# One memory set for the two plain groups of each feed-forward block, squares added by transfers, and h's low part two steps later

## What is computed

```python
def rms_norm_2(x, gain):
    xf = x.astype(jnp.float32)
    inv = lax.rsqrt(jnp.mean(xf * xf, axis=-1, keepdims=True) + NORM_EPS)
    return (xf * inv).astype(x.dtype) * gain

def swiglu(h, w_gate, w_up, w_down):
    return (jax.nn.silu(h @ w_gate) * (h @ w_up)) @ w_down
...
    x = x + jnp.square(jax.nn.relu(h2 @ w_up[l])) @ w_down[l]
...
    for l in range(DEPTH_2):
        x = x + 0.5 * swiglu(rms_norm_2(x, ffn1_norm[l]), ffn1_wg[l], ffn1_wu[l], ffn1_wd[l])
        ...
        x = x + 0.5 * swiglu(rms_norm_2(x, ffn2_norm[l]), ffn2_wg[l], ffn2_wu[l], ffn2_wd[l])
    return rms_norm_2(x, final_norm)
```

## Time and profile before

| | |
|---|---|
| median of 3 runs | 2504.01 us (2500.72 to 2505.83) |
| the profiled execution | 2501.46 us, its span 2499.3 us |
| busy in the span | PE 2427.9, PE weight loads 2158.8, DVE 1822.6, ACT 1269.4, POOL 195.3 us |
| granted TensorE clock, mean | 0.989 of full speed |

### The profile page before, as it was taken

How to read it: one execution, slowest core, us unless ns; L and a number is a source line. 1 busy time by engine, 2 the same in 40 slices (tenths; PEclk the granted TensorE clock), 3 DMA queues, 4 the chain that set the end, 5 groups by cost and what they waited for, 6 DMA issues and landing times.

```text
span 2499.3 us, 36547 instructions
## 1 busy us (share of the span) xinstructions
PE 2427.9 (97%) x14620; PEld 2158.8 (86%) x14620; DVE 1822.6 (73%) x2639; ACT 1269.4 (51%) x2023; POOL 195.3 (8%) x199
## 2 busy tenths in 40 slices
PE   9999998999979999999999999989999999999999
PEld 7878888999859999978889999889999788899998
DVE  7742477777679878675688777788877766887874
ACT  6677354444354544357454444554444465544443
POOL 2231010000030000012100000100000121000001
PEclk9999999999999999999999999999999999999999
DMA  7655442333322333236323333222332363233331
GB/s 204 151 124 126 118 135 85 102 102 100 100 71 79 107 102 102 68 106 156 109 84 95 102 102 102 98 89 93 102 102 77 109 152 110 85 102 102 102 101 68
DMA packets 103640, 263.76 MB, mean 106 GB/s; under 512 B 9648, under 2 KB 12976, under 8 KB 103088
## 3 DMA queue, kind: packets, MB, share of 16 engines
q1 hardware_dynamic: 94848, 233.57, 29.8%
q0 software_dynamic: 8624, 27.86, 5.5%
HBM read 234.56 MB, written 2.19 MB: 95 GB/s over the span
## 4 chain that ended last, share of the span: by engine, by line
PE 73%; DVE 12%; ACT 6%; issue 5%; DMA 3%; POOL 1%; SPq 0%; POOLq 0%; DVEq 0%; ACTq 0%
PE bank L1107 12%; PE bank L1108 12%; PE bank L1109 12%; PE bank L1155 12%; PE bank L1156 11%; PE bank L1157 11%; DVE w_raw_lo L1600 2%; DVE slot_lo L1600 2%; DVE x L1864 1%; ACT w_hi L1315 1%; PE bank L1171 1%; PE bank L1186 1%; DMA w_raw<-w_out_dram 1%; DVE rms_inv L1760 1%; ACT z L1303 1%
## 5 line engine op out<-in xcount | busy, mean ns | idle before, releaser
L1361 ACT ACTIVATE slot_hi<-slot_raw 128x1024 fp32r<-128x1024 f32 (+1 forms) x396 | 365.2, 952 | 144.3 <-DVE slot_raw L1646 115.8
L1600 DVE TENSOR_TENSOR slot_lo<-slot_raw,slot_hi 128x1024 fp32r<-128x1024 f32 (+1 forms) x396 | 427.1, 1100 | 4.1 <-ACT slot_hi L1361 4.1
L1155 PE MATMUL bank<-hs_hi,slot_hi 128*128 128x256 f32 x1504 | 426.1, 283 | 0.1
L1157 PE MATMUL bank<-hs_hi,slot_lo 128*128 128x256 f32 x1504 | 426.2, 283 | 0.0
L1156 PE MATMUL bank<-hs_lo,slot_hi 128*128 128x256 f32 x1504 | 426.1, 283 | 0.0
L1107 PE MATMUL bank<-act_hi,w_hi 128*128 128x512 f32 x960 | 380.3, 396 | 7.8 <-DVE w_raw_lo L1600 7.8
L1108 PE MATMUL bank<-act_lo,w_hi 128*128 128x512 f32 x960 | 380.2, 396 | 0.0
L1109 PE MATMUL bank<-act_hi,w_raw_lo 128*128 128x512 f32 x960 | 374.6, 390 | 0.0
L1155 PE MATMUL bank<-h_hi,slot_hi 128*128 128x256 f32 x1128 | 322.8, 286 | 39.2 <-DVE slot_lo L1600 35.8
L1379 ACT ACTIVATE part_a<-bank 128x256 f32<-128x256 f32 x188 | 71.8, 382 | 531.0 <-PE bank L1157 530.4
L1864 DVE SCALAR_TENSOR_TENSOR x<-bank,x 128x512 f32<-128x512 f32 x280 | 192.3, 687 | 191.3 <-PE bank L1109 190.0
(11 more groups left out here) (263 smaller groups left out, 4345.7 us busy)
## 6 DMA issues: line engine op xcount, KB each, us to landing
slot_raw<-ffn_wg_dram SPq DMA_DIRECT2D x88, 512.0 KB, 4.1
slot_raw<-ffn_wu_dram SPq DMA_DIRECT2D x88, 512.0 KB, 4.1
w_raw<-ffn_wd_dram SPq DMA_DIRECT2D x88, 512.0 KB, 3.7
w_raw<-w_in_dram SPq DMA_DIRECT2D x67, 512.0 KB, 3.6
w_lo<-w_raw POOLq DMA_DIRECT2D x43, 512.0 KB, 4.7
slot_raw<-w_up_dram SPq DMA_DIRECT2D x32, 512.0 KB, 4.4
w_raw<-w_down_dram SPq DMA_DIRECT2D x32, 512.0 KB, 3.6
w_raw<-w_out_dram SPq DMA_DIRECT2D x24, 512.0 KB, 3.7
```

Of the source, the lines that this page charges most:

```text
L1155: engine.matmul(to, slot_hi[:, g % 2, slot, lhs], hi, start=opens, stop=False, skip_group_check=True)
L1157: product = engine.matmul(to, slot_lo[:, g % 2, slot, lhs], hi, start=False, stop=closes, skip_group_check=True)
L1361: engine.activation(span_of(slot_hi, n, name), span_of(slot_raw, n, name), ACT.Copy).then_inc(signals["s_hi"].s, 1)
L1600: engine.tensor_tensor(lo, value, hi.bitcast(F32), ALU.subtract).then_inc(signals[event].s, 1)
```

## The change

Three things are changed.

**Memory sets.** `set_of` puts a stage's first group in the other set than its number says, so both plain groups lie in set 1, and the third group has set 0 for itself. Set 1 has seven places: the first group takes three of them and, for its fourth part, a place in the last quarter of `hs_raw`/`hs_hi`/`hs_lo` (`lead_x`), and the second takes the other four. The step j = 3 of `mix` then has to wait for the first output of the first group, and is placed later (slots 2, 8, 16). In `out_projection` all seven loads of the three groups are issued behind the first result, and the three are prepared behind results 2, 3 and 4. Between two feed-forward stages the third group of the next one is prepared during the last Strassen group.

**Squares.** In stages 1 to 7 the squares of tiles 2 to 7 are no longer added by POOL. POOL issues accumulating transfers into `square_sum` (even tiles) and `square_odd` (odd tiles), and DVE adds the two (`square_fold`) five slots behind the last tile; `sum_split` follows seven slots behind it instead of four. The scaled squares of stage 2 are still added by POOL.

**h's low part.** `h_rest` (DVE) is a job of its own, two slots behind `h_tile`.

```diff
--- before.py
+++ after.py
...
 PARTS = {"first": (B11, 2), "last": (B22, 2), "mixed": (T2, 2), "b21": (B21, 1)}
-PLAIN_PARTS = {"plain_a": (B11, 2), "plain_b": (B22, 2)}
-PARTS.update(PLAIN_PARTS)
-PLAIN_SLOT = ((B11, B21), (B12, B22))
+LEAD_SLOTS = (((0, None), (2, 4)), ((1, 6), (3, 5)))
+LEAD_PARTS = (("lead_a", (0, 3, 2)), ("lead_b", (4, 5, 1))), (("lead_a", (1, 4, 2)), ("lead_b", (5, 7, 1)))
...
-        if m == 0:
+        if m == 0 or m == 1 and 0 < s < FINAL:
             self.add("square_first", (s, m))
+        elif 0 < s < FINAL:
+            self.add("square_add", (s, m), None, self.z(f"square_added{m % 2}", (s, m)))
+            self.sig[f"square_added{m % 2}"].will((s, m))
+            if m == KT - 1:
+                self.later(5, "square_fold", s)
         else:
             self.add("square" if s > 0 else "square_zero", (s, m), None, self.z("square_sum", (s, m)))
 
     def norm_tile(self, s, m):
         self.add("h_tile", (s, m))
+        self.later(2, "h_rest", s, m)
         self.square(s, m)
         if s in MLP_STAGES and m == 1:
             self.mix(s, 0, 4)
         if m == KT - 1 and s in SPLIT_SUMS:
-            self.later(4, "sum_split", s)
+            self.later(7, "sum_split", s)
...
         n = self.begin_block(s)
...
-            if m < 2:
-                self.load("a", n + m)
-                self.load("b", n + m)
-            elif m == 2:
-                self.prepare_ahead(0)
+            if m == 0:
+                for part, ahead in (("a", 0), ("b", 0), ("x", 0), ("a", 1), ("b", 1), ("a", 2), ("b", 2)):
+                    self.load(part, n + ahead)
+            elif 2 <= m < 5:
+                self.prepare(n + m - 2, 0)
             self.norm_tile(s, m)
...
-                self.sg.append(Group(stage, kind, pair, STEADY, pair * len(set(kind for kind, _ in kinds)) < LEAD))
+                at = len(self.sg)
+                self.lead_of.setdefault(stage, at)
+                self.sg.append(Group(stage, kind, pair, STEADY, at - self.lead_of[stage] if at - self.lead_of[stage] < LEAD else None))
         self.block_end = len(self.sg)
-        self.block_of[n] = s
-        self.block_of[n + 1] = s
+        for i in range(LEAD + 1):
+            self.block_of[n + i] = s
         return n
...
+    def set_of(self, n):
+        return 1 - n % 2 if self.sg[n].lead == 0 else n % 2
...
+    def loads_when(self, g, what):
+
+        group = self.sg[g]
+        ahead = self.sg[g + 1].lead if g + 1 < self.block_end else None
+        if group.lead == 0:
+            if what == "end":
+                self.load("a", g + 3)
+        elif group.lead == 1:
+            if what == "half":
+                self.load("b", g + 2)
+        elif ahead == 0:
+            if what == "P6":
+                self.load("a", g + 1)
+            elif what == "end":
+                for part, n in (("b", g + 1), ("x", g + 1), ("a", g + 2), ("b", g + 2)):
+                    self.load(part, n)
+        elif what in ("P6", "end"):
+            n = g + 4 if g + 2 < self.block_end and self.sg[g + 2].lead == 0 else g + 2
+            self.load("a" if what == "P6" else "b", n)
...
+        if self.sg[n].lead == 0:
+            steps = ((0, "s_hi", (n, "lead_a")), (1, "s_hi", (n, "lead_b")), (2, "s_hi", (n, "lead_x")),
+                     (2, "s_lo", (n, "lead_a")), (3, "s_lo", (n, "lead_b")), (4, "s_lo", (n, "lead_x")))
+        elif self.sg[n].lead == 1:
+            steps = ((0, "s_hi", (n, "lead_a")), (2, "s_hi", (n, "lead_b")), (2, "s_lo", (n, "lead_a")), (4, "s_lo", (n, "lead_b")))
...
+        if not group.plain:
+            if g + 1 < self.block_end and self.sg[g + 1].lead == 0:
+                self.prepare(g + 3)
+            else:
+                self.prepare(g + 1, 2 if self.sg[g - 1].lead == 1 else 8)
...
     def plain(self, g):
         group = self.sg[g]
-        order = [(n, k) for n in range(2) for k in range(KT - 2)] + [(n, k) for n in range(2) for k in (KT - 2, KT - 1)]
-        if self.pending_norm is not None:
+        order = [(n, k) for n in range(2) for k in range(KT)]
+        if group.lead == 0:
+            order = [(n, k) for n in range(2) for k in range(KT - 2)] + [(n, k) for n in range(2) for k in (KT - 2, KT - 1)]
             for j in range(1, HALF_K):
-                self.mix(group.stage, j, 6 * (j - 1) + 2)
+                self.mix(group.stage, j, (2, 8, 16)[j - 1])
...
                 self.add("p_last", (g, n))
+                if n == 0:
+                    self.loads_when(g, "half")
...
-        self.prepare_ahead(4)
+        self.prepare(self.groups_done, 5)
+        self.prepare(self.groups_done + 1, 9)
...
+            with ExitStack() as sums:
+                square_odd = sbuf("square_odd", [P, TOKENS], F32, sums)
...
+        def lead_weights(g, n, k):
+
+            slot = LEAD_SLOTS[plan.sg[g].lead][n][k % 2]
+            j = k // 2
+            if slot is None:
+                return hs_hi[:, j, HALF_K - 1, 0:P], hs_lo[:, j, HALF_K - 1, 0:P], "lead_x"
+            part = "lead_a" if k % 2 == 0 else "lead_b"
+            return slot_hi[:, plan.set_of(g), slot, j * P:j * P + P], slot_lo[:, plan.set_of(g), slot, j * P:j * P + P], part
...
+                    hi, lo, part = lead_weights(g, n, k)
+                    pe.wait_ge(*done("s_lo", (g, part)))
...
                     to = (x_bank, yz_bank)[n][g % 2][:, :]
-                    engine.matmul(to, slot_hi[:, g % 2, slot, lhs], h_hi[:, k, :], start=k == 0, stop=False)
-                    engine.matmul(to, slot_hi[:, g % 2, slot, lhs], h_lo[:, k, :], start=False, stop=False)
-                    product = engine.matmul(to, slot_lo[:, g % 2, slot, lhs], h_hi[:, k, :], start=False, stop=job == "p_last")
+                    engine.matmul(to, hi, h_hi[:, k, :], start=k == 0, stop=False)
+                    engine.matmul(to, hi, h_lo[:, k, :], start=False, stop=False)
+                    product = engine.matmul(to, lo, h_hi[:, k, :], start=False, stop=job == "p_last")
...
                     act.wait_ge(*done("mix_4", key))
+                    if j == HALF_K - 1:
+                        act.wait_ge(*done("p_mm", (plan.lead_of[s], 0)))
                     engine.activation(hs_hi[:, :, j, :], h_mixed[:, :, :], ACT.Copy).then_inc(signals["mix_hi"].s, 1)
...
-                    square(key, square_sum[:, :], m, signals["squared"])
-
-                elif job in ("square", "square_zero", "square_last"):
+                    square(key, (square_sum, square_odd)[m][:, :], m, signals["squared"])
...
-                elif job == "h_tile":
+                elif job == "h_rest":
...
                 elif job == "s_t13":
                     n = key
...
+                    if n > 0 and plan.sg[n - 2].lead == 1:
+                        v.wait_ge(*done("p_mm", (n - 2, 1)))
...
+                elif job == "square_fold":
+                    v.wait_ge(*done("square_added0", (key, KT - 2)))
+                    v.wait_ge(*done("square_added1", (key, KT - 1)))
+                    engine.tensor_tensor(square_sum[:, :], square_sum[:, :], square_odd[:, :], ALU.add).then_inc(signals["square_sum"].s, 1)
...
+                elif job == "square_add":
+                    s, m = key
+                    pool.wait_ge(*done("squared", key))
+                    if m > 3:
+                        pool.wait_ge(*done(f"square_added{m % 2}", (s, m - 2)))
+                    engine.dma_start((square_sum, square_odd)[m % 2][:, :], z[zs % Z_RING][:, :], accum_op=ALU.add).then_inc(signals[f"square_added{m % 2}"].s, 16)
...
+                    n, part = key, job[-1]
...
+                    if part == "x":
+                        set_was_free(sp, n, 1, ("P3",))
+                        engine.dma_start(hs_raw[:, :, HALF_K - 1, 0:P], group_source(n)[:, 3, :].rearrange("p (k n) -> p k n", n=P)).then_inc(event, 16)
+                    elif part == "a":
+                        if lead == 1:
+                            set_was_free(sp, n, 1, ("P3",))
+                        elif n >= 3 and plan.sg[n - 3].lead == 0:
+                            sp.wait_ge(*done("p_mm", (n - 3, 1)))
+                        else:
+                            set_was_free(sp, n, 1, ("P6",))
+                        first = B11 if lead is None else LEAD_SLOTS[lead][0][0]
+                        engine.dma_start(slot_raw[:, at, first:first + 3:2, :], group_source(n)[:, 0:2, :]).then_inc(event, 16)
...
-                        engine.dma_start(slot_raw[:, n % 2, B22:B21 + 1:B21 - B22, :], group_source(n)[:, 2:4, :]).then_inc(b_landed[n % 2].s, 16)
+                        if lead is None and n >= 2 and plan.sg[n - 2].lead == 1:
+                            sp.wait_ge(*done("p_mm", (n - 2, 0)))
+                            sp.wait_ge(*done("p_mm", (n - 3, 1)))
+                        else:
+                            set_was_free(sp, n, 1, ("P3",))
+                        if lead == 0:
```

(5 more changed lines are left out.)

131 lines of the change are left out of this document (76 added, 55 removed).

## The result

The changed kernel takes 2515.69 us (median of 4 runs, 2514.85 to 2516.42) against 2502.7 us for the kernel before on the same chip. The ratio is 1.0051, 95% interval 1.0035 to 1.0067: **slower by 0.5%**, where 1.2% faster was forecast (2473 us, range 2454 to 2491). The profiled execution has a span of 2514.6 us, 15.3 more than before.

What follows compares the result with a forecast made beforehand. PE was taken as the bound, with about 71 us idle plus low-clock time to recover. Removed 61 us, added 30.3: net −30.7 on the profiled 2501.46 gives 2471, as a median 2473 us; range 2454 to 2491.

Steps and rivals of the forecast that it cites:

- Third groups, removed: Third groups of stages 1, 2, 4, 5, 7: PE's waits for `slot_lo` go, −34.96 us, and −11 of low clock.
- Wait at P4: Third groups' P4: PE newly waits for ACT's copy `part_b`, behind the fourth group's first `slot_hi` split; 15.4 us in all.
- the 6.9 us for low clock: Behind the new P4 waits: 2.5 us in stage 2, 1.7 in stage 1, 0.9 each in three stages.
- Tails: Ends of stages 1, 2, 4, 5: `w_raw_lo` no longer slowed by POOL's adds, −10.6 and most of −4.5; +4 left over.
- D, the landing of a square: Time for a 256 KB accumulating square transfer to land, taken as 3.7 us; range 2.9 to 4.7.
- 4 us over eight norms: Cost of squares by transfer at the norm sums: 0.5 us in four, about 1 in the two before mixers.
- nearly no shift: Norm chain from last square to the sum's matmul: 5.7 us by transfer against 5.46 before, where it is alone.
- the rival with the lead waits: Lead waits stay nearly as long, moved from P1 to P7 or P4; only the tails gain, some 11 us: 2493; chance 0.10 not given, 0.08.
- My rival with slow transfers: Squares' landing decides: net gain cancelled at D = 6.6 us, 2528 us at D = 8.3; chance 0.05.
- issued stages ahead: Third group's loads and splits, moved behind the output projection's first results or into the last Strassen group, delay no one.
- h's low part: `h_lo` made two slots later: costed at nothing; 0.75 us a stage if the covering weight products ran out.

Runs made afterwards that it cites:

- the run with squares on POOL and all spread: Changed kernel with loads behind results 0, 1 and 2, preparation behind results 2, 4 and 6, and squares added by POOL again: 2485.3 us, 0.9926.
- the run above: The 2485.3 us kernel (loads spread, squares on POOL) with preparation behind results 1, 3 and 5, not 2, 4 and 6: 2485.17 us, 0.9922.
- the second run: Changed kernel with the output projections' loads for three groups issued behind results 0, 1 and 2, a group each, not all behind result 0: 2501.85 us.
- the spread runs: Changed kernel with loads behind results 0, 1 and 2 and preparation behind 2, 4 and 6: 2501.84 us; with squares on POOL too, 2485.3 us.

## Why the prediction was wrong

Two steps failed. The norms were given 4 us for the squares by transfer and took 26, and the third group's preparation was given no term for what it meets in the output projections and took 30. The other terms came out, or came out better.

*Third groups, removed: right, and more.* All five waits and their low clock went.

*Wait at P4: right in place and reason, sizes mixed.* Forecast 2.8, 7, 1.9, 1.75, 1.9 us; the timeline of PE shows

```profile
398.24 0.58 PE L1241 MATMUL bank<-h_hi,slot_hi 128*128 128x256 f32 x1 [2.89 <-ACT part_b L1469]
...
756.74 0.58 PE L1241 MATMUL bank<-h_hi,slot_hi 128*128 128x256 f32 x1 [3.45 <-ACT part_b L1469]
...
1296.14 0.38 PE L1241 MATMUL bank<-h_hi,slot_hi 128*128 128x256 f32 x1 [1.63 <-ACT part_b L1469]
```

and 1.69 and 1.64 in stages 5 and 7. Stage 2's came out at 3.45 by luck, because PE had lost 4.58 us earlier, at its norm; in the run with squares on POOL and all spread, where that wait is 2.33, it is 6.19. And the waits of 1.6 to 1.7 us left the clock at 1.00 (the first matmul behind them lasts 0.38, not 0.58 us), so half of the 6.9 us for low clock did not come. In all the third groups gave 33 us net where the forecast had 46 − 22.3 = 23.7.

*Tails: right in sum, partly by luck.* 10.1 us from the table, against 15.1 less 4. But stages 1 and 4, forecast at some 8.6, gave 3.9, with waits of 2.10 and 2.06 us for `w_raw_lo` left where I had about 1; stages 2 and 5, forecast at some 2.5, gave 6.2. POOL's add beside the split was a cause: with the adds alone away, `w_raw_lo` cost 3.0 us in the whole program and not 10.8. But the transfers were not needed to part the two: with the adds on POOL and h's low part two slots later most splits took 1.21 us as well, and the tails gave 8.4 us of 10.5.

*D, the landing of a square: right where I looked, wrong where I did not.* I took 3.7; the median is 3.5. The least of the 42 is 3.2, and the SWDGE section of "DMA: Bandwidth & Descriptors" in the Trainium skill would have had 2.6 (an estimate from its fit); the trace does not agree, with no square under 3.2. But the forecast took one D for all norms. It gave the two before mixers about 1 us each, for want of a plain group to cover the sum, and did not ask **what else is in flight at each**. In the tails ahead of the mixers the weights of the next projection and the far mask are: 4.5, 5.4 and 8.9 us (least, median, most) from 1070 to 1085. The section "Queues, rings and completion order" of "DMA: Bandwidth & Descriptors" in the Trainium skill says that a DMA engine takes turns between queues packet by packet. By that a square on its own queue would share the engines with the far mask rather than wait behind it. The trace goes with that as far as it can say: the mask, too, took longer beside the squares, 8.3 us against 5.6 with the squares on POOL. No run here separates sharing from waiting.

The first step that failed is "4 us over eight norms". Measured: 7.3 (stage 2), 11.2 (stage 3), 7.8 (stage 6). In stages 3 and 6 it was the landing, 8.9 and 8.5 us. In stage 2 it was the sum itself: "nearly no shift" set D + 2.0 = 5.7 against the 5.46 us of the earlier trace rows, but those end at a matmul that waited for nothing, so they hold slack. Where PE did wait, the chain before was 1.73 us, and by transfer it is 4.11, both without the two splits, which stage 2 has not. (The 4 us themselves are the sum over six norms, 0.5 in four and 1 in two, and the rival with the lead waits left them out: by its own terms it comes to 2497, not 2493.) My rival with slow transfers had this mechanism and put it at 0.05, because I judged it by the 4.7 us median of the weights' transfers in the earlier trace rows; its 8.3 us in the earlier trace rows was the telling figure.

*The third group's preparation: the larger failure.* This is the second step that failed. The forecast's sentence was that these loads and splits are "issued stages ahead (…), where DVE is 73% busy and no one waits for them". The 73% is an average over the program; in an output projection DVE and ACT form a closed loop, residual, `h_hi`, square, `w_hi`, `w_raw_lo`, residual, of 4.1 to 4.4 us a result against PE's 5.44. Its slack is 1.0 us a result at 4.4, some 8 us over the eight, and two groups' splits take most of it (in the run above 8.9 − 4.4 and 7.3 − 4.4, 7.4 us). The third adds 9.4 − 4.4 = 5 us. And the seven loads take 9.2 us, so that weights come after PE needs them. Neither has a term in my sum. Measured: 30 us in three output projections. About half of that is the loads (14 us back in the second run, with preparation unmoved). What the spread runs leave at the norm sum, 3.7 us each and its clock, is the loop.

*h's low part: right beside the transfers, where it gave nothing.* That it would by itself take the split away from POOL's add, and so make the transfers all but needless, I did not see.

*Net.* Terms forecast and measured against the kernel before: third groups −23.7 and −33; tails −11 and −10; norms +4 and +26 (with +1.5 in stage 5, 28); output projections 0 and +30. The sum is −31 and +15.

## What to carry to other kernels

When work is moved earlier to where "no one waits", write down the loop that runs there, its length per step against the bound engine's, and how much slack it has left after what it already carries; the mean busy share says nothing of that. And ask of every transfer that is put on a path, or ahead of one, what is in flight when it is issued, stage by stage: the same 256 KB landed in 3.2 us in one place and 8.9 in another. A small load with a distant deadline (the far mask) is the first thing to move. And before work is taken off an engine because it slows another, see whether one job moved in the order parts the two: here h's low part two slots later gave 8.4 of the 10.5 us in the tails with all 42 transfers away.
